# A macaron S5 and Conformer block on one core: both FFN down projections as seven products with four sums per side

## The reference

```python
def swiglu_ffn(h, w_up, w_down):
    gate, up = jnp.split(h @ w_up, 2, axis=-1)
    return (jax.nn.silu(gate) * up) @ w_down

def reference(x, ...):
    h = rms_norm(x, norm_ffn1_g[l])
    x = x + 0.5 * swiglu_ffn(h, w_ffn1_up[l], w_ffn1_down[l])
    h = rms_norm(x, norm_mix_g[l])
    ...
    h = rms_norm(x, norm_ffn2_g[l])
    x = x + 0.5 * swiglu_ffn(h, w_ffn2_up[l], w_ffn2_down[l])
    return rms_norm(x, norm_final_g)
```

## Time and profile before

| what | us |
|---|---|
| median of 3 runs (lowest, highest) | 2243.48 (2243.1, 2243.74) |
| the profiled execution, its own time | 2242.39 |
| its span, first to last instruction | 2240.6 |
| PE busy in the span | 2192.9 (98%) |
| DVE, ACT, POOL busy | 1620.6, 963.4, 620.6 |
| chain that ended last: PE, DVE, ACT, DMA | 84%, 8%, 3%, 3% |

### The profile page before, as it was taken

The page is one execution under the profiler, slowest core; times in us unless marked ns, Lnnn a source line. Parts: engine busy times, 40 slices in busy tenths (PEclk is TensorE's granted clock), DMA queues, the critical chain, the costliest instruction groups (busy, mean ns, idle before and its releaser), DMA issues.

```text
span 2240.6 us, 32120 instructions
## 1 busy us (share of the span) xinstructions
PE 2192.9 (98%) x10370; PEld 1811.8 (81%) x10370; DVE 1620.6 (72%) x2065; ACT 963.4 (43%) x1573; POOL 620.6 (28%) x720
## 2 busy tenths in 40 slices
PE   7999999999999999999999999999999999999998
PEld 6788888888888888888888788888878888887886
DVE  5867777755564999999998659454587787766667
ACT  5455555544554222222223224134355555544444
POOL 2888998700000000000000430000026663531000
PEclk9999999999999999999999999999999999999999
DMA  5223444367763345445435632553257765648654
GB/s 170 78 85 125 145 139 147 126 214 242 248 218 127 103 140 155 132 140 155 138 113 172 197 104 80 192 193 118 71 165 248 252 232 186 221 163 305 211 195 172
DMA packets 299581, 370.62 MB, mean 165 GB/s; under 512 B 26489, under 2 KB 198609, under 8 KB 299120
## 3 DMA queue, kind: packets, MB, share of 16 engines
q1 hardware_dynamic: 279280, 296.04, 41.6%
q0 software_dynamic: 19056, 69.42, 8.5%
q10 hardware_dynamic: 1168, 4.20, 0.5%
HBM read 259.73 MB, written 107.50 MB: 164 GB/s over the span
## 4 chain that ended last, share of the span: by engine, by line
PE 84%; DVE 8%; ACT 3%; DMA 3%; issue 2%; SPq 1%; DVEq 0%; ACTq 0%
PE PU L1347 10%; PE PU L1349 10%; PE PU L1348 10%; PE PU L1288 9%; PE PU L1290 8%; PE PU L1289 8%; PE PU L1227 3%; PE PU L1228 3%; PE PU L1229 3%; PE PD L1227 3%; PE PD L1229 3%; PE PD L1228 3%; PE PD L1423 1%; PE PD L1424 1%; PE PD L1425 1%
## 5 line engine op out<-in xcount | busy, mean ns | idle before, releaser
L1288 PE MATMUL PU<-Hhi,Whi 128*128 128x512 f32 x896 | 352.7, 394 | 2.6 <-DVE Hlo L2386 2.0
L1289 PE MATMUL PU<-Hlo,Whi 128*128 128x512 f32 x896 | 349.2, 390 | 0.0
L1290 PE MATMUL PU<-Hhi,Wlo 128*128 128x512 f32 x896 | 349.2, 390 | 0.0
L2365 DVE SCALAR_TENSOR_TENSOR XT<-XT,wq 128x1024 f32<-128x1024 f32 x240 | 313.2, 1305 | 8.2
L1288 PEld LDWEIGHTS PU<-Hhi,Whi 128*128 128x128 f32 x896 | 168.3, 188 | 40.8 <-issue 3.0
L1290 PEld LDWEIGHTS PU<-Hhi,Wlo 128*128 128x128 f32 x896 | 168.3, 188 | 35.0
L1289 PEld LDWEIGHTS PU<-Hlo,Whi 128*128 128x128 f32 x896 | 168.4, 188 | 34.8 <-issue 0.7
L1347 PE MATMUL PU<-Hhi,Dhi 128*128 128x512 f32 x480 | 187.2, 390 | 1.9 <-ACT s1b L1696 1.9
L1348 PE MATMUL PU<-Hlo,Dhi 128*128 128x512 f32 x480 | 187.0, 390 | 0.0
L1349 PE MATMUL PU<-Hhi,Dlo 128*128 128x512 f32 x480 | 186.9, 389 | 0.0
L1227 PE MATMUL PD<-Dhi,Ahi 128*128 128x512 f32 x352 | 138.4, 393 | 5.6 <-DVE Alo L2010 5.6
(11 more groups left out here) (416 smaller groups left out, 5218.2 us busy)
## 6 DMA issues: line engine op xcount, KB each, us to landing
d_act<-G SPq DMA_DIRECT2D x88, 256.0 KB, 2.1
XT<-in_w_ffn_down SPq DMA_DIRECT2D x88, 256.0 KB, 3.2
XT<-d_act SPq DMA_DIRECT2D x88, 256.0 KB, 3.4
Wraw<-in_w_ffn_up SPq DMA_DIRECT2D x80, 256.0 KB, 4.2
XT<-in_w_ffn_up SPq DMA_DIRECT2D x80, 256.0 KB, 4.4
Wraw<-in_w_in SPq DMA_DIRECT2D x32, 512.0 KB, 5.2
Wraw<-d_sb SPq DMA_DIRECT2D x55, 256.0 KB, 2.9
d_sb<-TAB POOLq DMA_DIRECT2D x21, 512.0 KB, 3.2
```

The source lines that it names most:

```text
L1288: mm(o_, Whi[s][:, side, k, :], Hhi[:, k, hs[h]], start=k == 0, stop=False)
L1289: mm(o_, Whi[s][:, side, k, :], Hlo[:, k, hs[h]], start=False, stop=False)
L1290: last = mm(o_, Wlo[s][:, side, k, :], Hhi[:, k, hs[h]], start=False, stop=k == KT - 1)
L2365: stt(CVb, z_, w_, CVb, ALU.mult, ALU.add).then_inc(m["conv"], 1)
```

## The change

Both down parts now use the same seven products and four sums per side.

- `FFN1` gets FI = 11 steps and seven products in place of four phases of 22 steps. Its loop in the instruction lists is written out. Its raw tiles lie in `WRd` and `WRa`, over `Whi1` and `Wlo1`, so SP may load them only when product 5 of the last pair of the up part is done (`u_prod`); before, they lay in XT.
- Product order `D_ORD` = 2, 1, 5, 6, 3, 7, 4 on two sets of four banks in turn. Phases 3, 4 and 5 (`D_GOES_ON`) begin without clearing, so products 6, 3 and 7 add onto the bank that holds 1, 5 and 1 + 6. Eight additions per bank (`D_TO`, 32 DVE operations in each FFN), where the first FFN had 4 and the second 12.
- The four sums of activations are made by DVE in the up part, from tiles that are still in SBUF (K0, K1, E1, E2, over XT[6] and XT[7]): for every two pairs `sum_even`, `sums_high` (two operations) and `sum_low`. SP stores them (`store_sums`), with three of the four quarters that d_act got before (`store_kept`).
- POOL only makes the sums of weights (`take_weights`, four operations for each of 11 takes) and those of the first, plain couple (`take_first`): 48 operations for each FFN. For the first FFN this stands ahead of the eight tables of the mixer.
- At the end of the first down part the last four steps go bank by bank, as they did in the second, and the first eight transposes for the mixer lie between.

The pieces below are, in order, the tables, the tiles, SP's `down`, POOL's `take_weights` and its place, a line of PE's `proj_step`, and DVE's sums and their places in `fast_ffn`.

```diff
-D_ORD = (3, 5, 7, 4, 1, 2, 6)
+D_ORD = (2, 1, 5, 6, 3, 7, 4)
+D_GOES_ON = (3, 4, 5)
+D_ROWS_AT = ((0, 4), (0, 7), (1, 2), (1, 6))
+D_TO = {1: ((0, 1, 1),), 2: ((0, 1, 1),), 3: ((0, 0, 1),), 4: ((1, 1, -1),), 5: ((1, 0, 1),), 6: ((0, 0, 1),),
+        7: ((1, 0, 1), (1, 1, 1))}
...
+    WRd = over("Whi1", 0, "WRd", [P, RING, HW])
+    WRa = over("Wlo1", 0, "WRa", [P, RING, HW])
...
+    K0, K1, E1, E2 = [XT[:, 6 + i // 2, (i % 2) * HW:(i % 2 + 1) * HW] for i in range(4)]
...
+        def down(S, behind):
+
+            if S is FFN1:
+                sp.wait_ge(u_prod, 7 * (NSP - 1) + POS[5])
+            else:
+                sp.wait_ge(u_lo, 7 * (UBASE[FFN2] + NSP - 1))
+            for t in range(RING):
+                load_product(S, 0, t)
+            r = NSP - 1
+            stores = {4: lambda: store_kept(S, r), 6: lambda: store_sums(S, r, (M_S1, M_S2, M_S4))}
+            for p in range(7):
+                for t in range(FI):
+                    if p or t >= RING:
+                        load_product(S, p, t)
+                    if p == 0 and t in stores:
+                        stores[t]()
+                    if (p, t) in D_ROWS_AT:
+                        rows_down(S, *D_ROWS[D_ROWS_AT.index((p, t))])
...
+        def take_weights(S, k):
+
+            (b12, b11), (b22, b21) = [halves(row) for row in at_take(k)]
+            loaded(S, k, 0)
+            t1, t3, t2, t4 = b11, b12, b22, b21
+            step(g.tensor_tensor(t1, b12, b11, ALU.subtract))
+            loaded(S, k, 1)
+            step(g.tensor_tensor(t3, b22, b12, ALU.subtract))
+            store_take(S, k, 0)
...
+            step(g.tensor_tensor(t2, b22, t1, ALU.subtract))
+            row_free(S, k, 0)
+            load_take(S, k + 1, 1)
+            step(g.tensor_tensor(t4, t2, b21, ALU.subtract))
+            store_take(S, k, 1)
...
+        takes(FFN1)
         for q in range(KT):
             tile_table(q)
...
-                mm(o_, hi, at4(df, slot), start=first, stop=False)
+                mm(o_, hi, at4(df, place(S, slot)), start=first and not goes_on, stop=False, skip_group_check=True)
...
+        def sum_even(S, r):
...
+            tt(E1, K0, K1, ALU.subtract).then_inc(u_sum, 1)
+        def sums_high(S, r):
...
+            tt(K1, K1, G[1][:, :], ALU.add).then_inc(u_sum, 1)
...
+            tt(E2, K1, K0, ALU.subtract).then_inc(u_sum, 1)
+        def sum_low(S, r, saved):
...
+            dve.wait_ge(act_saved[0], c * 32 + (saved[0] + 32))
+            tt(K0, G[0][:, :], E2, ALU.subtract).then_inc(u_sum, 1)
...
                 lo_w(S, coming, 5)
+                if not second(r):
+                    sum_low(S, after(r, -1), saved)
                 lo_w(S, coming, 2)
...
                 lo_w(S, coming, 7)
+                if second(r):
+                    sums_high(S, r)
                 comb_21(S, r)
                 lo_w(S, coming, 4)
+                if not second(r):
+                    sum_even(S, r)
...
+        down(FFN1, {(0, 5): lambda: sum_low(FFN1, NSP - 1, SAVED0[FFN1]), (3, 9): lambda: split_pair(R_MIX, 0), (5, 9): lambda: row_scale("nmx", 0),
...
```

More of the change, by code:

```diff
@@ L99, in after, with couple, second @@
     return p + n if isinstance(p, int) else (p[0], p[1] + n)
+def couple(S, r):
+    g, i = r if isinstance(r, tuple) else (0, r)
+    return g + (i + 2) // 2, g + (i // 2 + SUMS0[S])
+def second(r):
+    return (r[1] if isinstance(r, tuple) else r) % 2
 def step_at(S, p, t):
@@ L407, in one @@
                 behind[t]()
[L409 to L417, removed]
+        for t in range(S.steps):
             one(t)
@@ new lines, in load_take, with loaded @@
+        def load_take(S, k, i):
+            down = {FFN1: w_ffn1_down, FFN2: w_ffn2_down}[S][0]
+            if k < FI:
+                src = down[(2 * k + i) * P:(2 * k + i + 1) * P]
+            else:
+                for h in range(2):
+                    pool.wait_ge(act_saved[h], SAVED0[S][h] + 32)
+                src = d_act[i]
+            pool.dma_start(at_take(k)[i], src).then_inc(pool_ld[i], 16)
+        def loaded(S, k, i):
+            pool.wait_ge(pool_ld[i], (0 if i else TABLES0[S]) + 16 * (k + 1 + (0 if S is FFN1 else TAKES)))
@@ new lines, in take_first @@
+        def take_first(S, k):
+            (a11, a21), (a12, a22) = [halves(row) for row in at_take(k)]
+            loaded(S, k, 0)
+            loaded(S, k, 1)
+            s1, s3, s2, s4 = a22, a21, a11, a12
+            step(g.tensor_tensor(s1, a21, a22, ALU.add))
+            step(g.tensor_tensor(s3, a11, a21, ALU.subtract))
+            step(g.tensor_tensor(s2, s1, a11, ALU.subtract))
+            store_take(S, k, 0)
+            step(g.tensor_tensor(s4, a12, s2, ALU.subtract))
+            store_take(S, k, 1)
@@ L1006, in tile_table, with takes @@
+        def takes(S):
+            load_take(S, 0, 0)
+            load_take(S, 0, 1)
+            for k in range(FI):
+                take_weights(S, k)
+            take_first(S, FI)
+            for i in range(2):
+                row_free(S, FI, i)
         def tile_table(q):
@@ L1156, in _ @@
         pool.wait_ge(rd_lo, FFN2.z0)
         pool.wait_ge(u_lo, 7 * (UBASE[FFN2] + 2))
-        pool.wait_ge(t_lo, 8)
-        for k in range(2):
-            load_take(k)
-        for k in range(len(TAKES)):
-            take(k)
+        takes(FFN2)
     @block.tensor
@@ L1712, in silu_1 @@
             act.wait_ge(u_prod, q * 7 + POS[2])
[L1713 removed]
+            if second(r):
+                act.wait_ge(u_c, q * 7 + (C_ACT1 - 7))
+            elif isinstance(r, int) and r == 0:
+                act.wait_ge(act_saved[0], saved0[0] + 32)
+            else:
+                act.wait_ge(act_saved[0], couple(S, r)[0] * 32 + saved0[0])
+                act.wait_ge(u_sum, couple(S, r)[1] * 4)
             fn(g1b, PUf[0][:, :], ACT.Silu).then_inc(u_g1, 1)
@@ L2201, in comb_s16 @@
             dve.wait_ge(u_s1, q + 1)
-            dve.wait_ge(act_saved[1], number(r) * 16 + (saved1 + 32))
+            if second(r):
+                dve.wait_ge(u_c, q * 7 + (C_ACT2 - 7))
+            else:
+                first = isinstance(r, int) and r == 0
+                dve.wait_ge(act_saved[1], saved1[1] + 32 if first else (couple(S, r)[0] + 1) * 16 + saved1[1])
+                if not first:
+                    dve.wait_ge(u_sum, couple(S, r)[1] * 4)
             tt(s16b, s1b, PUf[1][:, :], ALU.add).then_inc(u_c, 1)
@@ L2222, in comb_22 @@
             dve.wait_ge(u_c, q * 7 + C_22)
-            tt(s16b, s16b, s5b, ALU.mult).then_inc(u_c, 1)
+            if second(r):
+                tt(s16b, s16b, s5b, ALU.mult).then_inc(u_c, 1)
+                return
+            dve.wait_ge(t_lo, 4 * (UBASE[S] // NSP) + 4)
+            if S is FFN2 or not isinstance(r, int) or r:
+                dve.wait_ge(sa_st, couple(S, r)[1] * 64)
+            tt(K1, s16b, s5b, ALU.mult).then_inc(u_c, 1)
         def comb_21(S, r):
```

482 lines of the change are left out of this document (223 added, 259 removed).

## The result

The change makes the kernel **slower**: the median is 2268.30 us (2260.15 to 2273.10, 4 runs) against 2243.61 for the kernel before in the same comparison, a ratio of 1.0104 with a 95% interval of 1.0074 to 1.0135. 2219 was forecast, with 2233 as the upper end. The profiled execution took 2273.1 us, with a span of 2271.3.

The account below looks back on a forecast made before the run. PE's own matmul work was taken to set nearly all the time. Terms -29.9 - 5 + 2.5 + 5 + 2 + 1 = -24.4 us against the profiled 2242.39 gave 2218.0, forecast as a median of 2219, range 2208 to 2233.

Parts of the forecast that it names:

- The matmuls: First down part: 924 matmuls in place of 1056, 132 fewer at 0.227 us each, 29.9 us less.
- Start of the second down part: Step 4's stall goes, step 7 stalls 2 us behind stores of sums: 5 us less (ends 7 less and nothing).
- Start of the first down part: Tiles now wait for product 5 of the last pair: 2.5 us more (ends nothing and 7.0).
- The step 7 chain: Down part starts: step 7's load queues behind three stores waiting for `sum_low`; 2 us stall taken at the second start.
- The sums in the up parts: DVE's added sums delay `comb_s16` where POOL works: 5 us more in all (ends 2 less and 46 more).
- Tables under the first down part, and its end: DVE's subtractions beside POOL's tables, 2 us more; the first down part's end going bank by bank, 1 us more.
- the first rival: DVE becomes the bound of the first down part, PE waiting each step until tables end: 2234 us, chance 0.15.
- Its sign, fewer than 170 matmuls in 40 us: PE's matmul starts between 460 and 575 us, in the first down part; would show DVE as its bound.
- The slower rival: Up parts: `sum_low` ahead of `comb_s16` makes PE wait 2.3 us in all 20 couples: 2260 us, chance 0.03.

Follow-up runs that it names:

- e12: The change, unaltered, measured again in a second comparison: 2265.73 us against 2243.52 for the kernel before, ratio 1.0090.
- e3: The change with SP issuing the last pair's stores behind step 6's load and the stores of sums behind step 8's, both down parts: 2253.64 us, ratio 1.0048.
- e4: The change with `sums_high` placed behind `comb_21` and the last low part (in the last pair, step 3's split): 2253.85 us, ratio 1.0057.
- e1: The change with DVE's four sums of activations working on 8 columns in place of 512: 2233.80 us, ratio 0.9955.
- e7: e5 with every POOL operation of the takes in four parts of 128 columns: 2220.55 us, ratio 0.9894.
- e9: The change with nothing altered but POOL's operations of the takes, in four parts of 128 columns: 2231.37 us, ratio 0.9951.
- e5: The change with both e3's later stores and e4's later `sums_high`: 2238.81 us, ratio 0.9979.
- e6: e5 with POOL's takes of the second FFN made to wait for a place in the couple: 2237.22 us, ratio 0.9974.

## Why the prediction was wrong, step by step

The forecast was 24.4 us less, the profiled execution took 30.7 more. Of these 55 us, 31 lie in the up parts, 16 at the start of the first down part and 3 at that of the second; the rest is in small differences that no term of the sum covers.

- **The matmuls: right.** 132 fewer, each at 0.227 us. The groups are three of 176 and three of 132, not six of 154 as I wrote, the sum is 924.
- **Start of the second down part: the chain right, its gain too high: 5 us less forecast, 2.3 measured.** Step 4's wait is gone and step 7 waits 2.07 us behind the stores of sums; slower matmuls behind it and a shorter wait make 4.5 us in all. In e12, the same kernel again, steps 7 and 8 wait and the start loses 6.9 us, so nothing is gained on the 6.8 of before. I had priced the wait alone and not the slower matmuls that follow it. e3 shows that the order of SP's list is the whole of it.
- **Start of the first down part: wrong, 2.5 us forecast, 18.7 measured, over the upper end of 7.0.** I counted a load, copies and subtractions against 8.2 us of room, and gave this start a little more than the other. The step that failed is that `comb_21` was left out of the chain: it had moved behind two added operations, and both ACT's copy of step 3 and SP's stores, with steps 5 and 6 behind them, wait for it. e3 shows SP's part; e4 frees step 3 and makes step 4 wait for the same two operations. The step 7 chain, which I did see, cost 7.3 us and not 2.
- **The sums in the up parts: wrong, 5 us forecast, about 36 measured** (17.0 + 15.7 + 3.4 in the second start; within the ends of -2 and 46). I asked what `sum_low` alone adds ahead of `comb_s16`, 2.3 us at most less 1.2 of slack, and left what `sums_high` pushes back without a number. The runs show that the four sums and the stretched rows around them add up over a couple, since DVE has no idle time left there to catch up in. A couple that waited beside takes lost 4 to 9 us, not 0.4 or 0.8. I also carried one price over all of POOL's work; beside tables in the first up part nearly nothing was lost, beside takes nearly all. The trace of before had this to read: a row with two SBUF inputs took 1.13 us as a mean beside the tables (200 to 435 us) and 1.50 beside takes (1680 to 1790). And I left out the clock after a wait, 1.5 to 2.9 us in five of the six.
- **Tables under the first down part, and its end: right in size.** 2 + 1 us forecast, 2.9 more than before in the rest of that part, of it 0.6 in the last 30 us. The split rows took 1.17 and 1.28 us as a mean (1.1 taken), and from 560 to 600 us DVE is busy for 38.17 of 40 with PE at its full pace. The margin was thin: from 542.8 to 553.6 us the two subtractions took 3.5 to 3.8 us a step, where PE needs 2.72, and PE waited three times, 0.6 to 1.0 us. That is the first rival, for a few steps only. Its sign, fewer than 170 matmuls in 40 us, was there (99 and 162), but the 99 are the start's stall. Other runs with the same tables lost 1.0 to 7.2 us in this rest, so that the size agrees is partly luck. The last table left POOL at 601.21 us, not near 575, and d_tab was read at 714.28: cover enough.
- **The slower rival** had the right engine and the right line, L2251, and with 2260 nearly the time. Its condition was wrong: not all 20 couples at 2.3 us, but the six beside takes at 4 to 9, and the start of the first down part besides. That the time came near is luck: 19 of the us are not in the up parts at all. It had a chance of 0.03, because I weighed it by its own mechanism alone and against windows of before, in which DVE still had slack.

The Trainium skill, page "SBUF — State Buffer", section "Who interferes with whom", states that a VectorE instruction with two SBUF inputs contends with a GpSimd instruction that reads SBUF, that the lock is exclusive, and that issue order decides who blocks. The prediction set this beside the sum and went by 1.1 us as a mean and 2.3 as the longest. On the hold the trace agrees: DVE's rows end 0.56 to 0.57 us behind POOL's in the fence above, 8 columns take as long as 512 in e1, and quarters cut the hold in e7. On the order of issue the rows cannot tell, since the row of the engine that was held begins first (279.15 against 279.52).

## What to carry to other kernels

Before work is moved to DVE beside a busy GpSimd, follow the chain on DVE from one point that PE waits for to the next, with each two-SBUF operation at its length plus one GpSimd operation as an estimate (0.69 + 1.30 = 2.0 us here; the mean beside takes was 1.44, the longest row 2.4); an average share of busy time of 75% hides a chain that has none left. If it doesn't fit, cut GpSimd's operations into short ones first: that cost POOL 0.9 us an operation and won 34 us (e12 to e9), but only where POOL has time to spare. At a seam between two parts, look at what a queue stands at (here 9.2 us for two stores that nobody needed soon), and put loads ahead of it.

## What the runs showed of the hardware that was not expected

- A DVE operation whose row begins up to 0.56 us ahead of POOL's is held too, where a DMA issue of POOL lies just ahead: such rows are the longest, up to 2.4 us, and all 19 rows over 2.1 us beside the takes are of this kind. Beside an issue with no operation to follow they take 0.69.
- A change can cost steadiness: the kernel before lay within 0.4% in all its comparisons, the changed one between 2258.5 and 2273.1. That the takes of POOL meet the pairs differently from run to run would explain it, and fits the first up part of e5 and e6; no run was made to show it.
- What stays open: of the losses in the mixer and before 115 us, 1.9 and 1.6 us more than before, no run looked for the cause; and the start of the second up part lost 7.8 us with the change, 4.0 to 4.9 where the sums or POOL's operations were short, and 4.4 to 7.3 in e3 to e6, too wide a spread to say what of it is DVE's (its 3.4 us are in the 36 above).
